# Prompt attention scores: one 384-column product for the low key parts, and keys loaded for each unit

## What is computed

```
qb = q.reshape(B, nb, BLOCK, N_KV_HEADS, GQA_GROUP, HEAD_DIM)
kcat = concatenate([concatenate([zeros, kb[:, :-1]]), kb], axis=2)
s = einsum('bnqkgd,bnskd->bnkgqs', q, k) * HEAD_DIM ** -0.5
mask = (rel >= 0) & (rel <= WINDOW) & (kpos >= 0)
e = exp(s - m);  pr = e / (sum(e) + exp(sink - m));  o = einsum(pr, v)
```

## Time and profile before

| | us |
|---|---|
| median of three runs | 1164.6 |
| the profiled execution's own time | 1165.09 |
| its span | 1163.3 |
| TensorE (PE) busy in the span | 1156.3 |
| VectorE, ScalarE, GpSimd busy | 563.9, 395.9, 407.7 |

### The profile page before, as it was taken

How to read it: one execution, slowest core, us unless ns; L and a number is a source line. 1 busy time by engine, 2 the same in 40 slices (tenths; PEclk the granted TensorE clock), 3 DMA queues, 4 the chain that set the end, 5 groups by cost and what they waited for, 6 DMA issues and landing times.

```text
span 1163.3 us, 20002 instructions
## 1 busy us (share of the span) xinstructions
PE 1156.3 (99%) x7656; PEld 1143.1 (98%) x7656; DVE 563.9 (48%) x1045; ACT 395.9 (34%) x954; POOL 407.7 (35%) x191
## 2 busy tenths in 40 slices
PE   8999999999999999999999999999999999999998
PEld 8999999999999999999999999999999999999998
DVE  5566774112556566564726465832363451163322
ACT  6433334233766767666110010321321030031112
POOL 4433332333212222223333344335432532374310
PEclk9999999999999999999999999999999999999999
DMA  9425466313455555652611111072223232412211
GB/s 303 168 73 149 141 165 181 94 46 87 132 154 158 153 154 134 166 148 74 218 54 51 37 50 36 23 276 76 92 75 124 82 124 77 135 65 64 65 38 56
DMA packets 145791, 130.83 MB, mean 112 GB/s; under 512 B 49039, under 2 KB 134439, under 8 KB 145727
## 3 DMA queue, kind: packets, MB, share of 16 engines
q1 hardware_dynamic: 131063, 106.21, 30.0%
q10 hardware_dynamic: 14664, 23.74, 7.1%
HBM read 94.82 MB, written 37.12 MB: 113 GB/s over the span
## 4 chain that ended last, share of the span: by engine, by line
PE 99%; DMA 1%; SPq 0%; DVE 0%; issue 0%; DVEq 0%
PE ps L684 75%; PE ps L822 11%; PE ps L933 2%; PE ps L708 2%; PE ps L1092 1%; PE ps L964 1%; PE ps L947 1%; PE ps L784 1%; PE ps L698 1%; PE ps L968 1%; PE ps L951 1%; PE ps L1061 1%; DMA xr<-in_x_prompt 1%; PE ps L888 0%; PE ps L868 0%; PE ps L1040 0%
## 5 line engine op out<-in xcount | busy, mean ns | idle before, releaser
L684 PE MATMUL ps<-m_hi,w_hi 128*128 128x352 f32 x1704 | 556.1, 327 | 0.1
L684 PE MATMUL ps<-m_lo,w_hi 128*128 128x352 f32 x1704 | 548.1, 322 | 0.0
L684 PE MATMUL ps<-m_hi,w_lo 128*128 128x352 f32 x1704 | 369.8, 325 | 0.0
L684 PEld LDWEIGHTS ps<-m_hi,w_hi 128*128 128x128 f32 x1704 | 320.9, 188 | 1.3 <-issue 0.5
L684 PEld LDWEIGHTS ps<-m_lo,w_hi 128*128 128x128 f32 x1704 | 320.7, 188 | 0.0
L597 POOL TENSOR_TENSOR w_hi<-raw_a,w_one 128x1024 fp32r<-128x1024 f32 x41 | 78.9, 1923 | 683.4 <-PE ps L684 371.4
L684 PEld LDWEIGHTS ps<-m_hi,w_lo 128*128 128x128 f32 x1704 | 289.8, 188 | 0.0
L599 POOL TENSOR_TENSOR w_lo<-raw_b,w_hi 128x1024 fp32r<-128x1024 f32 x41 | 111.1, 2709 | 3.2
L599 POOL TENSOR_TENSOR w_lo<-raw_a,w_hi 128x1024 fp32r<-128x1024 f32 x41 | 104.1, 2539 | 3.2
L822 PE MATMUL ps<-w_lo,m_hi 128*128 128x256 f32 (+1 forms) x360 | 99.4, 282 | 0.0
L822 PE MATMUL ps<-w_hi,m_hi 128*128 128x256 f32 x320 | 92.3, 288 | 0.0
(11 more groups left out here) (248 smaller groups left out, 1429.9 us busy)
## 6 DMA issues: line engine op xcount, KB each, us to landing
raw_a<-in_w_in SPq DMA_DIRECT2D x25, 512.0 KB, 3.7
raw_b<-in_w_in SPq DMA_DIRECT2D x25, 512.0 KB, 4.6
qk_d<-qkst ACTq DMA_DIRECT2D x20, 512.0 KB, 5.6
gate_d<-gst ACTq DMA_DIRECT2D x16, 528.0 KB, 3.4
gin<-gate_d SPq DMA_DIRECT2D x16, 528.0 KB, 3.6
qt<-qk_d SPq DMA_DIRECT2D x64, 128.0 KB, 3.5
kt<-qk_d SPq DMA_DIRECT2D x96, 64.0 KB, 2.5
vt<-v_d SPq DMA_DIRECT2D x84, 64.0 KB, 2.2
```

What stands on the lines that cost most here:

```text
L684: last = nc.tensor.matmul(ps[:, 3 * parity + c, 0:CH], w, x[:, k, CH * c:CH * c + CH], start=(k == 0 and w is wh and x is src_hi), stop=(k ...
```

## The change

Each scores step becomes one matmul of 384 columns and two of 192. The 384-column product takes new weights, q_high, which hold the high query parts of head pair 0 on partitions 0 to 63 and of pair 1 on 64 to 127, against two new key versions side by side: part 1 has the low key part on the upper half of the partitions 0 to 63 and zeros below, part 2 has zeros on 0 to 63 and the low key part on 64 to 127. The two products with part 0 stay. The product of low query with low key is no longer summed.

The ring of keys goes. kt holds, in two slots, the blocks t - 1 and t of one unit, loaded anew for each unit by two DMAs of 128 KB (64 KB for t = 0). q_high is loaded by four DMAs of 32 KB in runs of 256 B. So `load_q_k` issues eight DMAs for each unit. VectorE zeroes all of kt (1536 elements a partition in place of 1024), and SP waits for that before its first load_q_k. A gap of 1024 elements moves tiles in SBUF.

```diff
-            kt = sb("kt", [P, NKV, 2, 3, P], F32R, scope=s3)
+            kt = sb("kt", [P, 2, 3, 2 * P], F32R, scope=s3)
+            k_gap = sb("k_gap", [P, 1024], scope=s3)
+            q_high = sb("q_high", [P, 2, 2, 2, HD], F32R, scope=s3)
@@ load_q_k
-                tok, kv = bass.ds(t * P, P), m % 4
+                kv = m % 4
                 for a in range(2):
                     src = qk_d[G * kv:G * kv + G, :, bass.ds(t * P + HD * a, HD)]
                     sp.dma_start(qt[:, m % 2, a, :, :].bitcast(F32), src.rearrange("g p n -> p g n"))\
                         .then_inc(unit_loaded[kv], 16)
-                for slot in ((2, 0) if m < 4 else (1,)):
-                    for half in range(2):
-                        sp.dma_start(kt[HD * half:HD * half + HD, kv, :, slot, :].bitcast(F32),
-                                     qk_d[NH + kv, :, tok].rearrange("(s e) n -> e s n", s=2))\
-                            .then_inc(unit_loaded[kv], 16)
+                    for b in range(2):
+                        heads = qk_d[G * kv + 2 * b:G * kv + 2 * b + 2, 0:HD, bass.ds(t * P + HD * a, HD)]
+                        sp.dma_start(q_high[HD * b:HD * b + HD, m % 2, a, :, :].bitcast(F32),
+                                     heads.rearrange("g e n -> e g n")).then_inc(unit_loaded[kv], 16)
+                first = isinstance(t, int) and t == 0
+                seen = slice(0, P) if first else bass.ds(t * P - P, 2 * P)
+                for half in range(2):
+                    dst = kt[HD * half:HD * half + HD, m % 2, 0:2 + half:1 + half, P if first else 0:2 * P]
+                    sp.dma_start(dst.bitcast(F32), qk_d[NH + kv, :, seen].rearrange("(s e) n -> e s n", s=2))\
+                        .then_inc(unit_loaded[kv], 16)
@@ before the first load_q_k on SP
+            sp.wait_ge(zero_done, 1)
@@ scores
-                    pe.wait_ge(unit_loaded[kv], i * 160 + (96 if m < 4 else 160))
+                    pe.wait_ge(unit_loaded[kv], t * 128 + 128)
-                k0 = (P if m < 4 else 0) + HD * s
+                seen = slice(HD * s, HD * s + KW)
+                nc.tensor.matmul(ps[:, bank, :].rearrange("p (b n) -> p b n", b=2)[:, :, 0:KW],
+                                 q_high[:, slot, s, :, :].rearrange("p g n -> p (g n)"), kt[:, slot, 1:3, seen],
+                                 start=True, stop=False)
                 for b in range(2):
-                    for part in range(2):
-                        keys = kt[:, kv, part, :, :].rearrange("p s n -> p (s n)")[:, k0:k0 + KW]
-                        last = nc.tensor.matmul(ps[:, bank, 256 * b:256 * b + KW],
-                                                qt[:, slot, s, 2 * b:2 * b + 2, :].rearrange("p g n -> p (g n)"), keys,
-                                                start=(part == 0), stop=(part == 1))
+                    last = nc.tensor.matmul(ps[:, bank, 256 * b:256 * b + KW],
+                                            qt[:, slot, s, 2 * b:2 * b + 2, :].rearrange("p g n -> p (g n)"),
+                                            kt[:, slot, 0, seen], start=False, stop=(b == 1))
@@ VectorE, last sample group
-                    v.memset(kt[:, :, :, 1, :].bitcast(F32), 0.0).then_inc(zero_done, 1)
+                    v.memset(kt[:].bitcast(F32), 0.0).then_inc(zero_done, 1)
```

More of the change, by code:

```diff
@@ L919, in round_of, with scores @@
                 return 6 + (att_bank(kind, m, first) + s) % 2
-            def scores(u, m, i, s, first=False):
+            def scores(u, m, t, s, first=False):
                 slot, kv = m % 2, m % 4
@@ L975, in attention_half @@
                 after, between = {k0: [], k0 + 1: [], k0 + 2: [], k0 + 3: []}, {}
-                after[k0].append(lambda: scores(u, m, i, 0, first and m == 0))
-                after[k0 + 1].append(lambda: scores(u, m, i, 1, first and m == 0))
+                after[k0].append(lambda: scores(u, m, t, 0, first and m == 0))
+                after[k0 + 1].append(lambda: scores(u, m, t, 1, first and m == 0))
                 if not first or m >= 1:
```

## The result

The changed kernel took 1174.6 us, the median of four runs (1173.6 to 1175.2); the kernel before, measured beside it, 1164.6 (1163.95 to 1164.9, four runs). The ratio is 1.0085, with an interval of 1.0069 to 1.0101: 10 us slower, where 3.7 were forecast and 1173.5 was the upper end. The profiled execution took 1175.2 us with a span of 1173.4, so it is compared with the 1163.3 of before.

A forecast was written before the change was run, and what follows sets the result against it. TensorE was taken to bound the kernel, with SP becoming slower in the loop. Terms: -3.1 (TensorE) + 1.5 (start) + 5.3 (loop) = +3.7 us, 1168.3 us against the median 1164.6; range 1163.0 to 1173.5.

The forecast's parts named there:

- The gain on TensorE: Scores steps: 0.40 us in place of 0.44, one uncovered weight load less, 3.1 us saved over 64 steps.
- Two strips: Rival at the 384-column product: two strips cost as much as two products, gain gone, 1171.4 us; chance 0.04.
- The 4.5 us: Scores steps: estimated gain by the Trainium skill's weight-load rule, step of 376 ns, 64 x 0.07; the trace's row was preferred.
- The form of q_high: SP's q_high issues: 64 partitions in two runs like kt, so priced at kt's 607 ns median.
- SP keeps up: Rival in the loop: q_high issues take 0.38, units under 7.6, no loop stall, 1161.5 us; chance 0.09.
- The start: Values products of units 0 and 1: stalls of 0.7 and about 0.8 us, together 1.5, between 0.6 and 2.2.
- Units 2 to 7 as cover: Before the loop: unit 4's two kt DMAs and wait absorb remaining delay; v keeps 1.5 us of slack for the loop.
- SP's unit in the loop: SP in the loop: 7.8 us a unit plus 0.27 to the next, 8.1, against TensorE's 7.97 with the gain.
- SP is stretched: Rival in the loop: slow issues come more often, 8.4 us a unit adds 4.8, 1173 us; chance 0.13.
- The landing of v: Loop v loads: the last lands 2.2 us after its issue starts, leaving 3.1 us of slack before the change.
- the transfers come late: Rival: v lands 1.3 us later behind 256 B runs, once at start and once in loop, 1170.9 us; chance 0.05.
- the loop's 5.3 us of stalls: Loop values products: SP slower by 3.5 us a turn, 7.0 in two, less 1.5 slack and some 0.2.

The follow-up runs named there:

- the version with both edits: The changed kernel with SP's loop over units 8 to 23 written out and v issued before q and k: 1161.7 us, ratio 0.998.
- the q_high kernel over 128 partitions: The changed kernel with each q_high load made 128 partitions and one run, same bytes, prompt scores wrong: 1163.4 us, ratio 0.999.
- With constant addresses: The changed kernel with SP's loop over units 8 to 23 written out, same DMAs, sizes and order: 1164.1 us, ratio 0.9998.
- the kernel with the small store: The changed kernel with each 528 KB gate store cut to its first 16 columns (8 KB), y outputs wrong: 1171.0 us, ratio 1.0048.
- another order: The changed kernel with v of unit u - 2 issued before q and k of unit u: 1170.5 us, ratio 1.0053.
- q_high by head: The changed kernel with each q_high DMA filling 128 partitions from heads of both pairs, data right: 1194.9 us, ratio 1.0267.

## Why the prediction was right and wrong, point by point

- **What bounds the kernel.** Right. SP, which waited for TensorE, became the one that TensorE waits for, at the values products and because of v.
- **The gain on TensorE.** Right: 3.1 us forecast; the version with both edits has it, 1161.7 against 1164.8. Two strips cost no more than one run of 384 columns (0.17), so that rival fell. The 4.5 us were mis-worked: they set the step of before as measured, about 0.45, against a step of after by the rule. With the rule of the Trainium skill, "TensorE: Matmul & The Clock Gate" (LDWEIGHTS; Back-to-back issue gap), on both sides, an estimate, the step is four loads of 107, 428 ns, before and 376 after, and the gain 0.052 a step, 3.3 us. The runs, 3.1, agree with that.
- **The form of q_high.** Right: 0.607 us in the median, as kt. The rival "SP keeps up" had the right point of decision. With 0.45 an issue the loop's waits do disappear, but this DMA doesn't have that price.
- **The start.** Right in sum: 0.78 and 0.59 us at the products of units 0 and 1, 1.4 against 1.5.
- **Units 2 to 7 as cover.** Wrong. I had a unit with constant addresses at 6.8 us and 1.5 us of slack of v at the loop's start. Units 3 to 7 took 7.1 to 8.2, and the product of unit 5, still ahead of the loop's loads, waited 0.82. So the loop began with next to none of the slack: v of unit 6 landed 0.42 us before its product started. The step that failed is the price of such a unit, taken from a mean pitch of 0.64 in unit 2 without the slow issues. The wait at unit 5 isn't theirs alone: its v also landed 2.5 us after the end of its issue, beside a gate store, where 1.65 is usual.
- **SP's unit in the loop.** Mis-sized: 8.1 with its gap forecast, 8.0 + 0.30 = 8.3 measured. Its parts without a slow issue were right (units 19 and 20, 7.66 and 7.80 long, the chunk 1.24); the difference is the slow issues, which the rival "SP is stretched" named, a longer pause between two issues in some units (0.51 us in unit 8 and 0.44 in unit 12, which took 8.1 without a slow issue), and a gap of 0.30 for 0.27. Over the 15 units in question 0.2 each is about 3 us.
- **The landing of v.** Wrong. I took 2.2 us from the page, a median, as if it were the value. The waits came from the tail, 5.4 us at most here. I had "the transfers come late" as a rival with 1.3 us, each once, and put it down to q_high's short runs. Those do no harm (the q_high kernel over 128 partitions has the same runs and no wait in the loop); the cause is the gate store on another queue. The same stores were there before the change, but they didn't make v late in the loop: there the v loads landed 1.6 to 1.7 us after the end of their last issue, all but one (unit 11, 2.7, with no gate store under way). With constant addresses it is 1.65 to 1.85 for those that the loop loads. The times of the stores tell why. In the loop of the kernel after they start 0.8 to 3.5 us before the last v issue of an odd unit ends, and v lands late (only the store at unit 13 starts after that end, and its v is on time). Before the change and with constant addresses a store either starts at most 0.3 us before that end, or after it, or has landed by 0.6 us after the first v issue started. So the stores meet the v loads where SP has fallen behind.
- **The clock.** Not in the forecast. 1.5 us in the profiled execution; what it is in the others isn't shown.

The term that failed is the loop's 5.3 us of stalls. In its place the products of units 5 to 21 waited 10.4 us, and the clock took 1.5. The mechanism, SP as the slower of the two and the wait at the values products, was right; the slack at the loop's start, SP's unit and the landing of v were each put too well.

The forecast lacked 6.4 us (3.7 against 10.1). By the kernel with the small store, late landings and what follows them (the idle clock, and SP's own waits of about 1.6 us at units 15 and 16 while TensorE stood still) are some 4 of them. SP's unit, about 3 us by the sum above, and the lost slack, about 1, make up more than the rest. These don't add up exactly: with the small store SP's unit is also 0.15 shorter, 2.4 us over the 16 units, which was counted with both. This division is an estimate from single executions. Each of these terms made a queue with a deficit of 3.5 us a turn worse, and none of them was evened out. My range ended where one such surprise ended, and three came together, with the same sign.

What stays open is why an issue sometimes takes 1.0 to 1.5 us. It happens with constant and with computed addresses, and the small gate store took none of these away: among the issues of q, k and v from 289 to 545 us six take over 1.0 us with it, and five in the kernel after. Those of 0.8 to 1.0 us went, from nine to none. Both kernels have them, before too (up to 1080 ns).

## What to carry to other kernels

Before moving work to a queue that "only issues", multiply its issues by their price from the trace and compare the sum with the pace of the engine that it feeds. If the queue comes out slower, even by 5% as here, don't count on its slack: in this kernel the deficit met every late landing and slow issue at full cost, and took most of the faster engine's gain with it. A load's slack is to be held against its longest landing, not against the median; and for a queue that is short by little, constant addresses or a form of DMA with a shorter issue helped more here than another order, which by itself won 4 of 10 us and moved the wait.

## What the runs showed of the hardware

- The issue time of a DMA on SP depends on its form, not on its bytes: 0.61 us in the median for 64 partitions in two runs, at 32 KB (q_high) and at 128 KB (kt); 0.45 for 128 partitions in one run, at the same 32 KB and the same runs of 256 B; 0.56 for 128 partitions from a source of two blocks. The Trainium skill, "DMA: Bandwidth & Descriptors" (Issuing engines are not separate DMA queues), says that the sequencer's time to start a DMA is usually small relative to the DMA itself. In this trace it isn't small enough: with eleven issues a unit, most of them 0.61 us for a load that lands 2.3 us after the start of its issue (q_high, median), they are what bounds the loop.
- From the end of an issue to the next are 0.04 us with constant addresses and mostly 0.09 to 0.20 with computed ones, up to 0.51. Over a unit of eleven issues without a slow one that is 6.7 to 7.1 against 7.6 to 8.1 us, which decides whether the loop waits, though most single issues of 128 partitions are shorter with computed addresses (0.38 to 0.46 against 0.59).
- After a wait of TensorE of 2.4 us most of the next 4 us ran at the lower clock level, after another of 2.6 none. With q_high by head it was so after four waits of 2.6 to 3.0 us, and not after a fifth of 2.6.
- A 528 KB store on ScalarE's queue delayed the v loads on SP's: in the kernel after they landed 2.2 to 4.75 us after the end of their last issue where a store had started 0.7 to 3.5 us before that end, and 1.4 to 1.75 with the store cut to 8 KB.
